# Squares of two norms added up on GpSimd, with one sum over partitions per norm and half, and six up tiles by halves

## The reference, cut to what matters

```python
for l in range(DEPTH):                       # 2 layers
    ...
    y = mixer_block(h, ...)                  # ends in: outs @ w_o, 1024 x 1024
    x = x + gt1 * rms_norm(y, norm_g[l, 1])              # norm "y1"
    h = rms_norm(x, norm_g[l, 2]) * (1.0 + sc2) + sh2    # norm "h2"
    y = jnp.square(jax.nn.relu(h @ w_up[l])) @ w_down[l] # 1024 -> 4096 -> 1024
    x = x + gt2 * rms_norm(y, norm_g[l, 3])
```

## Time and profile before

| | us |
|---|---|
| median of 3 runs | 2361.47 (2356.61 to 2362.36) |
| the profiled execution, its own time | 2361.32 |
| its span | 2359.1 |
| TensorE busy | 2097.7 (89% of the span), 9668 matmuls |
| VectorE busy | 1145.5 (49%) |
| ScalarE busy | 812.0 (34%) |
| GpSimd busy | 52.4 (2%), 49 instructions |

### The profile page before, as it was taken

The page is one execution under the profiler, slowest core; times in us unless marked ns, Lnnn a source line. Parts: engine busy times, 40 slices in busy tenths (PEclk is TensorE's granted clock), DMA queues, the critical chain, the costliest instruction groups (busy, mean ns, idle before and its releaser), DMA issues.

```text
span 2359.1 us, 27293 instructions
## 1 busy us (share of the span) xinstructions
PE 2097.7 (89%) x9668; PEld 1593.1 (68%) x9668; DVE 1145.5 (49%) x1886; ACT 812.0 (34%) x1353; POOL 52.4 (2%) x49
## 2 busy tenths in 40 slices
PE   6797888996688989988799999998997989999996
PEld 4684446885355557864597888775874578888774
DVE  4665547766776573246444323325236445423423
ACT  2424443234322233225444323223224444323411
POOL 0003000000200000000000000000000000000000
PEclk9898999998789999987799999999997889999998
DMA  7483006774001162200021222222220021222221
GB/s 259 174 302 122 0 1 249 271 277 169 7 7 58 45 242 72 107 36 1 14 95 54 91 105 89 89 89 90 96 82 1 1 72 52 91 101 95 89 89 71
DMA packets 46832, 233.36 MB, mean 99 GB/s; under 512 B 4983, under 2 KB 6519, under 8 KB 29720
## 3 DMA queue, kind: packets, MB, share of 16 engines
q1 hardware_dynamic: 46744, 232.22, 27.2%
HBM read 229.97 MB, written 2.10 MB: 98 GB/s over the span
## 4 chain that ended last, share of the span: by engine, by line
PE 81%; DVE 10%; ACT 4%; issue 3%; DMA 1%; SPq 0%; DVEq 0%; ACTq 0%
PE banks L1734 17%; PE banks L1736 17%; PE banks L1735 17%; PE banks L1924 3%; PE banks L1946 2%; PE banks L1772 2%; PE banks L1761 2%; PE banks L1762 2%; PE banks L1763 2%; PE banks L1860 1%; PE banks L2181 1%; PE banks L2089 1%; PE banks L2100 1%; PE banks L2028 1%; PE banks L2153 1%
## 5 line engine op out<-in xcount | busy, mean ns | idle before, releaser
L1061 DVE TENSOR_TENSOR w_low<-w_raw,w_high 128x1024 fp32r<-128x1024 f32 x226 | 276.4, 1223 | 493.7 <-ACT w_high L458 492.9
L1734 PE MATMUL banks<-h_high,w_high 128*128 128x512 f32 x1240 | 484.4, 391 | 19.2 <-DVE w_low L1061 16.1
L1735 PE MATMUL banks<-h_low,w_high 128*128 128x512 f32 x1240 | 483.6, 390 | 0.0
L1736 PE MATMUL banks<-h_high,w_low 128*128 128x512 f32 x1240 | 483.4, 390 | 0.0
L458 ACT ACTIVATE w_high<-w_raw 128x1024 fp32r<-128x1024 f32 x228 | 239.7, 1052 | 192.4 <-PE banks L1736 151.8
L1734 PEld LDWEIGHTS banks<-h_high,w_high 128*128 128x128 f32 x1240 | 233.5, 188 | 70.1 <-DVE w_low L1061 13.6
L1736 PEld LDWEIGHTS banks<-h_high,w_low 128*128 128x128 f32 x1240 | 233.5, 188 | 48.9
L1735 PEld LDWEIGHTS banks<-h_low,w_high 128*128 128x128 f32 x1240 | 233.6, 188 | 48.2
L1734 PE MATMUL banks<-hidden_high,w_high 128*128 128x512 f32 x512 | 207.8, 406 | 0.0
L1735 PE MATMUL banks<-hidden_low,w_high 128*128 128x512 f32 x512 | 200.4, 391 | 0.0
L1736 PE MATMUL banks<-hidden_high,w_low 128*128 128x512 f32 x512 | 200.4, 391 | 0.0
(11 more groups left out here) (422 smaller groups left out, 3062.3 us busy)
## 6 DMA issues: line engine op xcount, KB each, us to landing
w_raw<-in_wt SPq DMA_DIRECT2D x129, 1024.0 KB, 4.8
mod_raw<-in_wmod SPq DMA_DIRECT2D x144, 512.0 KB, 5.1
cmp_w<-in_cmp_w SPq DMA_DIRECT2D x2, 2048.0 KB, 8.5
x<-in_xT SPq DMA_DIRECT2D x1, 2048.0 KB, 11.1
dft<-in_dft SPq DMA_DIRECT2D x1, 2048.0 KB, 10.7
out_x<-x SPq DMA_DIRECT2D x1, 2048.0 KB, 7.2
hy_w<-in_hy_w SPq DMA_DIRECT2D x8, 192.0 KB, 3.2
tab_attn<-in_tab_attn SPq DMA_DIRECT2D x1, 1216.0 KB, 10.0
```

What stands on the lines that cost most here:

```text
L1061: v.tensor_tensor(low[:, :, :].rearrange("p k c -> p (k c)"), RAW[b // 2][:, b % 2, :], high[:, :, :].rearrange("p k c -> p (k c)").bitcas ...
L1734: mm(out, high[:, k, :], H[:, kk, :], start=start and k == 0, stop=False)
L1735: mm(out, high[:, k, :], L[:, kk, :], start=False, stop=False)
L1736: last = mm(out, low[:, k, :], H[:, kk, :], start=False, stop=stop and k == KT - 1)
```

## The change

- GpSimd adds the 8 squared slices of one norm and half into a 128x256 buffer (`SUMS`, in four parts): 7 additions, 28 a layer, in an order written out for its queue. A square waits for the addition of the slice before it in its slot in place of a sum. TensorE does one matmul of ones on the finished buffer (`square_total`): 4 a layer in place of 32. They stand inside half tiles: y1 a in half tile b 0 ahead of slice 5, h2 a in b 4 ahead of slice 1, y1 b in up tile 0 ahead of slice 5, h2 b in up tile 4 ahead of slice 1.
- Six up tiles are done by halves in place of four (`HALF_UPS`). Tiles 4 and 5 use the buffers WH, WL. Their half b comes behind the interleaved four. Two full tiles follow, written out, then a loop of 2 x 4.
- The high and low parts and the steps of the norms change places in the queues of ScalarE and VectorE. ScalarE's `hidden` is defined further up, unchanged.

The diff, cut to its core:

```diff
-    FIRST_UP = [tuple(at(BIG_AT + o * KB + 4 * KB * i, [P, KT, P], f32r, name="w_up") for i in range(2)) for o in (16, 24, 48, 56)]
+    FIRST_UP = [tuple(at(BIG_AT + o * KB + 4 * KB * i, [P, KT, P], f32r, name="w_up") for i in range(2)) for o in (16, 24, 48, 56)] + [
+        (WH[u], WL[u]) for u in range(2)]
+    HALF_UPS = len(FIRST_UP)
     HS = S // 2
+    SUMS = at(MOD_AT + 4 * KB, [P, 4 * HS], name="square_sums")
...
                     if t >= 2:
-                        act.wait_ge(*when(f"y1_ss_a.{t - 2}"))
+                        act.wait_ge(*when(f"y1_acc_a.{max(t - 2, 1)}"))
                 else:
                     act.wait_ge(w_used, 4 * (Q + 6) + t + 1 + PRIME)
-                    act.wait_ge(*when(f"y1_ss_b.{t - 2}" if t >= 2 else f"y1_ss_a.{t + 6}"))
+                    act.wait_ge(*when(f"y1_acc_b.{max(t - 2, 1)}" if t >= 2 else "y1_acc_a.7"))
...
             root_half("y1", "a", 4)
+            y_out("b", 0)
             high_of(Q + 8, 0, FIRST_UP[0][0])
-            y_out("b", 0)
             x_squares("a", (0, 1))
             y_out("b", 1)
-            x_squares("a", (2, 3, 4))
+            x_squares("a", (2, 3))
+            high_of(Q + 8, 1, FIRST_UP[1][0])
+            x_squares("a", (4,))
             y_out("b", 2)
-            high_of(Q + 8, 1, FIRST_UP[1][0])
-            x_squares("a", (5, 6))
+            x_squares("a", (5, 6, 7))
             y_out("b", 3)
-            x_squares("a", (7,))
             up_high(2)
             root_half("h2", "a", 6)
             y_out("b", 4)
-            highs_half("a", (0, 1, 2))
+            highs_half("a", (0, 1))
+            up_high(3)
+            highs_half("a", (2,))
             y_out("b", 5)
-            highs_half("a", (3, 4, 5))
+            highs_half("a", (3, 4, 5, 6, 7))
             y_out("b", 6)
-            highs_half("a", (6, 7))
-            up_high(3)
+            for u in range(2):
+                high_of(Q + 9, u, WH[u])
             y_out("b", 7)
             root_half("y1", "b", 5)
             first_hidden("a", 0)
-            x_squares("b", (0, 1, 2))
+            x_squares("b", (0, 1))
             first_hidden("a", 1)
-            x_squares("b", (3, 4, 5))
+            x_squares("b", (2, 3, 4, 5))
             first_hidden("a", 2)
             x_squares("b", (6, 7))
             first_hidden("a", 3)
-            high_of(Q + 9, 0, WH[0])
             root_half("h2", "b", 7)
-            highs_half("b", range(KT))
-            for u in range(4):
+            highs_half("b", (0, 1))
+            first_hidden("a", 4)
+            highs_half("b", (2, 3, 4, 5))
+            first_hidden("a", 5)
+            highs_half("b", (6, 7))
+            for u in range(HALF_UPS):
                 first_hidden("b", u)
-
-            def hidden(a, q, b, n, prev):
-
-                act.wait_ge(w_used, 4 * q + b + 1 + PRIME)
-                if prev:
-                    act.wait_ge(*prev)
-                nc.scalar.activation(RL[b % 2][:, :], bank(b), ACT.Relu).then_inc(taken, 1)
-                act.wait_ge(taken, 4 * q + b + 1 + PRIME)
-                nc.scalar.activation(SQ[b % 2][:, :], RL[b % 2][:, :], ACT.Square).then_inc(*did(f"relu{a}.{n}"))
+                if u >= 4:
+                    high_of(Q + 9, u - 2, WH[u % 2])
+            for b in (2, 3):
+                if b == 3:
+                    split_high(Q + 10, 0)
+                hidden(0, Q + 9, b, f"first{b + 4}", when("hid0_b.first5"))
...
+            def accumulate(tag, h, ks):
+                acc, slot = square_sum(tag, h), 2 * ("y1", "h2").index(tag)
+                for k in ks:
+                    pool.wait_ge(*when(f"{tag}_sq_{h}.{k}"))
+                    if k > 1:
+                        pool.wait_ge(*when(f"{tag}_acc_{h}.{k - 1}"))
+                    gp.tensor_tensor(acc, sq_slot(slot) if k == 1 else acc, sq_slot(slot + k % 2), add).then_inc(*did(f"{tag}_acc_{h}.{k}"))
+
+            accumulate("y1", "a", range(1, 8))
+            accumulate("h2", "a", (1,))
+            accumulate("y1", "b", (1,))
+            accumulate("h2", "a", (2, 3, 4))
+            accumulate("y1", "b", (2,))
+            accumulate("h2", "a", (5, 6, 7))
+            accumulate("y1", "b", range(3, 8))
+            accumulate("h2", "b", range(1, 8))
...
             for t in range(1, 8):
                 low_of(Q + 6 + t // 4, t % 4, KEPT[t])
-            branch_half("a", (2, 6))
-            low_of(Q + 8, 2, FIRST_UP[2])
+            branch_half("a")
+            for u in range(2):
+                low_of(Q + 8, u, FIRST_UP[u])
             norm_half("a")
-            low_of(Q + 8, 3, FIRST_UP[3])
+            for u in range(2, HALF_UPS):
+                low_of(Q + 8 + u // 4, u % 4, FIRST_UP[u])
             branch_half("b")
-            for u in range(4):
+            for u in range(3):
                 first_hidden("a", u)
-            low_of(Q + 9, 0, (WH[0], WL[0]))
             norm_half("b")
-            for u in range(4):
+            for u in range(3, HALF_UPS):
+                first_hidden("a", u)
+            for u in range(HALF_UPS):
                 first_hidden("b", u)
+                if u >= 4:
+                    low_of(Q + 9, u - 2, (WH[u % 2], WL[u % 2]))
...
+        def square_total(tag, h, b):
+            pe.wait_ge(*when(f"{tag}_acc_{h}.7"))
+            mm(bank(b, HS), ONES, square_sum(tag, h), start=True, stop=True).then_inc(*did(f"{tag}_ss_{h}.all"))
+
         def half_tile(out, weights, h, ready=None, at_k=None):
             high, low = weights
...
                 half_tile(bank(t % 4, HS), KEPT[t], 0, "mx3_lo" if t == 0 else None).then_inc(*did(f"y1_mm_a.{t}"))
-                if t:
-                    part_sums("y1", "a", 4, 0, (t - 1,))
             for t in range(8):
                 if t < 4:
                     pe.wait_ge(*when(f"y1_out_a.{t + 4}"))
                 else:
                     pe.wait_ge(taken, 4 * (Q + 6) + t - 3 + PRIME)
-                half_tile(bank(t % 4, HS), KEPT[t], 1, None, (lambda: part_sums("y1", "a", 4, 0, (7,))) if t == 0 else None).then_inc(w_used, 1)
-                if t:
-                    part_sums("y1", "b", 5, 0, (t - 1,))
-                if t in (2, 3):
-                    part_sums("h2", "a", 6, 2, range(4 * t - 8, 4 * t - 4))
-            for u in range(4):
+                half_tile(bank(t % 4, HS), KEPT[t], 1, None, {0: (5, "y1", "a", 4), 4: (1, "h2", "a", 6)}.get(t)).then_inc(w_used, 1)
+            for u in range(HALF_UPS):
                 pe.wait_ge(w_low, 4 * (Q + 8) + u + 1 + PRIME)
-                pe.wait_ge(taken, 4 * (Q + 8) + u - 3 + PRIME)
-                half_tile(bank(u, HS), FIRST_UP[u], 0, "h2_lo_a" if u == 0 else None, (lambda: part_sums("y1", "b", 5, 0, (7,))) if u == 0 else None).then_inc(*did(f"up_mm_a.{u}"))
-                if u >= 2:
-                    part_sums("h2", "b", 7, 2, range(4 * u - 8, 4 * u - 4))
+                if u < 4:
+                    pe.wait_ge(taken, 4 * (Q + 8) + u - 3 + PRIME)
+                else:
+                    pe.wait_ge(*when(f"up_out_a.{u - 4}"))
+                half_tile(bank(u % 4, HS), FIRST_UP[u], 0, "h2_lo_a" if u == 0 else None, {0: (5, "y1", "b", 5), 4: (1, "h2", "b", 7)}.get(u)).then_inc(*did(f"up_mm_a.{u}"))
             for k in range(KT):
                 pe.wait_ge(*when(f"h2_lo_b.{k}"))
                 for u in range(4):
                     if k == 0:
-                        pe.wait_ge(*when(f"up_out_a.{u}"))
+                        pe.wait_ge(*when(f"up_out_a.{u + 4 if u + 4 < HALF_UPS else u}"))
                     high, low = FIRST_UP[u]
                     mm(bank(u, HS), high[:, k, :], Hh[:, k, half(1)], start=k == 0, stop=False)
                     mm(bank(u, HS), high[:, k, :], Hl[:, k, half(1)], start=False, stop=False)
                     last = mm(bank(u, HS), low[:, k, :], Hh[:, k, half(1)], start=False, stop=k == KT - 1)
                     if k == KT - 1:
                         last.then_inc(w_used, 1)
+            for u in range(4, HALF_UPS):
+                pe.wait_ge(taken, 4 * (Q + 8) + u - 3 + PRIME)
+                half_tile(bank(u % 4, HS), FIRST_UP[u], 1).then_inc(w_used, 1)
+            for b in (2, 3):
+                tile(Q + 9, b, Hh, Hl).then_inc(w_used, 1)
             for a in range(2):
                 q0 = Q + 8 + 8 * a
-                with led.loop(pe, f"up{a}", 3 + a) as i:
+                with led.loop(pe, f"up{a}", 2 + 2 * a) as i:
                     for b in range(4):
-                        tile(i + q0 + 1 - a, b, Hh, Hl).then_inc(w_used, 1)
+                        tile(i + q0 + 2 - 2 * a, b, Hh, Hl).then_inc(w_used, 1)
```

More of the change, by code:

```diff
@@ L196, in rl_slot, with square_sum @@
     def rl_slot(u):
-        return RL[u // 2][:, half(u % 2)]
+        return (RL[0], RL[1], SQ[0])[u // 2][:, half(u % 2)]
+    def square_sum(tag, h):
+        n = 2 * ("y1", "h2").index(tag) + "ab".index(h)
+        return SUMS[:, n * HS:n * HS + HS]
     def part(T, k, h):
@@ L878, in _, with hidden @@
```

(45 more changed lines are left out.)

7 lines of the change are left out of this document (2 added, 5 removed).

## The result

The changed kernel takes 2341.0 us (median of four executions, 2338.6 to 2346.3) where the kernel before takes 2359.2 (four, 2356.6 to 2362.4): a ratio of 0.9934, with a 95% interval from 0.9915 to 0.9953. The forecast was 2344, the range 2327 to 2361.

A forecast was written before the change was run, and what follows sets the result against it. TensorE's own queue was taken as the bound; per layer 133.9 us without waits, 9.3 of waits and 2.0 of clock make 145.2 against 153.9, 17.4 less in all: forecast 2344 us, range 2327 to 2361.

The forecast's parts named there:

- Removed, 12.0 for 28 sums and 2.3 of waits for squares: TensorE's queue, per layer: 28 of 32 sums at 0.43 us go, and their waits for squares with them.
- First half, 0.8: First half's half tiles: TensorE waits three times 0.26 us for a late low part, which the sums used to cover.
- Waits for the sums, 3.7, 1.1 and 2.5: TensorE's waits in us per layer for the sums of h2 first half, y second half and h2 second half.
- its hold on VectorE: A GpSimd addition of 256 columns, priced at 0.73 us, was let hold VectorE (DVE) for 0.60.
- Relu of up tile 6 and the low part: TensorE waits 0.8 us for a late Relu before the second half's k = 0, 0.4 before the first full tile.
- Clock, 2.0: One clock loss of 2.0 us per layer, charged for the wait of 3.7; a second left open.
- 133.9: The new stretch per layer, second half tile of the output projection to the down projection, without any wait, in us.
- A: Rival: GpSimd and DVE don't hold each other at 256 columns; stretch 137.3, kernel 2328 us; chance 0.20.
- B: Rival: an addition of 256 columns costs 1.00 us like one of 384, holding DVE 0.87; kernel 2358; chance 0.18.
- C: Rival: at 1.22 us per addition the addition chain becomes the bound; kernel 2368, slower; decides from 1.07; chance 0.12.

The follow-up runs named there:

- tiles_only: The changed kernel with TensorE's 32 sums per layer back in place of GpSimd's additions, six up tiles by halves and new queue order kept: 2343.9 us.
- half_cols: The changed kernel with six of the seven additions per norm and half covering 128 of 256 columns: 2328.0 us.
- places alone: The changed kernel with only places changed: TensorE's h2 sums later, bank order, ScalarE and VectorE queue order; no work removed: 2323.8 us, ratio 0.9855.
- late_a: The changed kernel with TensorE's sum for h2's first half one half tile later (b 5 in place of b 4): 2336.6 us.
- extra: The changed kernel with a GpSimd product of 128 columns with ones behind each addition, which the next step waits for: 2364.0 us.
- sums_only: The kernel before with GpSimd's additions and one TensorE sum per norm and half, still four up tiles by halves: 2349.3 us.

## Why the prediction was right

The sum for one layer was 145.2 us for the new stretch; 145.4 and 145.3 were measured. That close a hit is partly luck, since the terms that were off cancelled.

- **Removed, 12.0 for 28 sums and 2.3 of waits for squares.** Right together. In the kernel before, 14 of the 32 sums stand alone at 0.43; the other 18 stand in four groups of five and four, which take 2.56, 2.98, 2.72 and 2.13. All 32 thus cost 16.4, four sums 1.7, and 14.7 went where 14.3 were expected. The 2.6 above 32 x 0.43 are the waits inside the groups, since the third sum of h2 needs a square whose slot the first one has to free. A group of five (rows of the kernel before: sums, and TensorE's next matmul; 2.98 is 0.13 + 2.79 + 0.30 less the usual 0.24):

```profile
1214.22 2.29 PE L2181 MATMUL banks<-sq,eye 128*128 128x256 f32 x8
1216.67 0.70 PE L2181 MATMUL banks<-sq,eye 128*128 128x256 f32 x2
1217.01 0.47 PE L1761 MATMUL banks<-h_high,w_kept 128*128 128x256 f32 x1
```

- **First half, 0.8.** Mis-sized, 1.4: from the second half tile at 1177.84 to the sum for y a at 1201.16 are 23.3 us, where 183 matmuls at 0.12 are 22.0. The low part is late three times, as forecast, but with stopping and starting (next point but one) this takes 0.41, 0.32 and 0.33 us in place of 0.26, and 0.4 more goes in starts at the other tiles.
- **Waits for the sums, 3.7, 1.1 and 2.5.** The right places and the right releaser, each too long: 2.87, 0.64 and 1.58. The addition was priced rightly (0.73, measured 0.74), its hold on VectorE a little high (0.60, measured about 0.55). Relu of up tile 6 and the low part: 0.8 and 0.4, measured 0.61 and 0.41.
- **What a wait costs beside its idle time.** A term that the sum lacked: 0.26 for each of these five waits, 1.3. Idle time counts from the end of the last matmul, 0.28 behind its start, where the next one would have started 0.12 behind it; and the first matmul after the wait holds the second back by 0.1. Three rows around the wait for Relu, 1.11 us where 0.24 are usual, with 0.61 idle:

```profile
1250.22 0.28 PE L2253 MATMUL banks<-h_high,w_up 128*128 128x256 f32 x1
1251.10 0.39 PE L2251 MATMUL banks<-h_high,w_up 128*128 128x256 f32 x1 [0.61 <-ACT sq L942]
1251.33 0.28 PE L2252 MATMUL banks<-h_low,w_up 128*128 128x256 f32 x1
```

- **Clock, 2.0.** One fall, with the longest wait, as said. It cost some 2.6: between the sums for h2 a and y b lie 16.4 us (1214.69 to 1231.71 - 0.64), where 0.43 and 108 matmuls are 13.4; of the 3.0 about 0.3 is the stop and start just named.

In all: 133.9, waits of 7.5, 1.3 for stopping and starting and 2.6 of clock are 145.3. Against the 9.3 and 2.0 of the sum the waits were 0.5 too dear and the clock 0.6 too cheap. tiles_only bears it out: its sums cost 13.7 more than four (15.4, the groups at their shortest), and 5.1 of waits for sums, 0.8 of stops, 1.4 in the first half and 2.6 of clock are gone, together 3.8 longer than the change; measured 3.7. The two parts, which the prediction never weighed apart, bring 4.9 and 3.9 a layer, and its own terms give the first: 4.2 + 2.0 - 0.6 - 0.8 - 0.4 = 4.4.

The rivals: A, with no hold, falls by VectorE's steps of 0.99 and 0.97. No run takes the hold away whole. half_cols, with additions of 0.46 that still hold (a step of 0.48 takes 0.69), also came to 2328, but that two numbers meet here is chance: its stretch is 141.1, where A had 137.3. B falls with the 0.74. C is real in its mechanism and lies at the price where it was put; the additions are just not that dear.

The rule of the Trainium skill that was weighed ("SBUF — State Buffer", "Who interferes with whom") holds here: steps of VectorE with two SBUF inputs stand still while an addition runs, a step of 0.42 for up to 0.57 of its 0.74. The estimate from the Trainium skill's "GPSIMD Engine Reference", section 3.1, 0.56 us for 256 columns, does not hold: the measured 0.74 decides. Scaling by columns leaves out a share that does not shrink with them (0.46 at 128, 0.74 at 256 columns).

## What to carry to other kernels

Moving small sums off the bottleneck engine pays less than their time there, since the chain through the slower engine turns into waiting: ask for each of them when its result is ready, and put the instruction that needs it no earlier in the bottleneck's queue. A wait costs about twice if the clock falls with it (2.87 and some 2.6 here), so several short ones are better than one long one, though each costs a little beside its idle time; here places alone brought 15 us in the two stretches, nearly as much as the 17 of the whole change. To see parts of less than 0.3%, compare one stretch of equal work in the traces, and trust medians of four executions only to some 4 us (the intervals of the table).

## What the runs showed of the hardware

- GpSimd's fp32 addition of two SBUF tensors on 128 partitions takes 0.46 us for 128 columns and 0.74 for 256, alone. VectorE's steps grow by 0.55 beside it, and the addition by up to 1.1 (1.8 in all) behind a low part of 1.22.
- TensorE's clock fell to half with waits of 2.05 (half_cols), 2.70 (late_a), 2.72, 4.12 and 7.88 (extra), 2.87, 3.91 and 5.37 us, the last two in sums_only. It stayed at full behind 1.58 in the changed kernel and 1.48 in late_a. The fall itself varied: in the repeat of the changed kernel the wait of 2.86 was followed by 0.96 for 0.8 us and by 0.50 for 3.4 us, and layer 1's stretch was 144.3 in place of 145.4.
- The fall does not need a load: it is there with a DMA share of 0.01 and 0.02 (extra).
- A wait inside TensorE's stream of 256-column matmuls cost 0.26 us more than the idle time before it.
